# A hybrid streaming encoder step on one core: the order of TensorE's and ScalarE's work inside a mixer slot

## The chip, the core and the metric

One Trainium2 chip, and of it one core. The kernel is one program on that core: TensorE (PE) multiplies, VectorE (DVE) and ScalarE (ACT) work element by element, GpSimd (POOL) does a few additions, SyncE (SP) issues the transfers. Each engine runs its own list of instructions in order, and the lists are tied together by semaphores alone. The metric is the time of one execution in microseconds on the device; the kernel before has a median of 2633.47 us over 3 runs (2633.35 to 2634.78).

## What is computed

One trunk layer of an encoder for a prompt of 1024 tokens and a sample of 64 tokens (with caches). Cut to what matters here:

```python
x = x + 0.5 * swiglu_ffn(x, *ffn1)
h = rms_norm(x, mix_g)
qa, ka, va, qb, kb, vb, fl = split(h @ w_in)            # heads, q and k normalized per head
o_a = band_sink_attention(qa, ka, va, bias, valid, sink)  # 8 heads on 2 key heads, window of 3 chunks of 64
o_b = forgetting_attention(qb, kb, vb, F, F, pos, pos)    # 8 heads, causal, F = cumsum(log_sigmoid(fl + b_f))
g_a, g_b = split(sigmoid(h @ w_gate))
x = x + (g_a * (o_a @ w_a) + g_b * (o_b @ w_b)) @ w_out
x = x + 0.5 * swiglu_ffn(x, *ffn2)
x = x + sigmoid(rms_norm(x) @ w_pg) * (p @ w_pp)
```

Both attentions are a softmax over scores plus a bias (or decay), times values. Dimensions: model 1024, feed-forward 2816, head 64.

## The kernel before

Tokens lie along the free axis, 1088 of them in three chunks of 364, 364 and 360 columns. Every dense float32 product is made of three products of split operands (high by high, low by high, high by low). The program is a first feed-forward, then the **mixer**, then a merge, a second feed-forward and a last gate. Only the mixer is touched; it lies between about 838 and 1319 us of the profiled span.

In the mixer, projection weights come in units of 128 output columns. One chunk of a unit takes 24 products (`PRODUCTS`, 8 blocks of the model by 3 ways). The mixer is cut into **slots** (`N_SLOTS` = 86), and all engines walk through the slots in the same order, each with its own code per slot: `mix()` in the TensorE, ScalarE and VectorE parts, and a loop on SP. Tables made ahead (`TAKEN`, `ITEM_AT`, `TURN_AT`, `VALUE_AT`, `ST_AT`) say what a slot holds:

- **unit products** (L658): slots 0 to 5 have 24, slots 6 to 25 have 21 or 22, slots 26 to 67 have 15 or 16, slots 68 to 81 have 10 or 11, slots 82 to 85 none. Slots 68 to 81 make the first merge gates and are called the gate stage here.
- **scores** of one attention item (L688): item g stands in slot 6+g. Items 0 to 19 belong to the sliding window (four head pairs of five items; of the five the first has a narrow part, the last is the sample with 64 rows). Items 20 to 75 belong to the forgetting attention, 14 per head pair; an item has at most 512 keys, and a row block of 128 queries with more keys takes two items, of which the second closes the softmax.
- **turns** (L707 and L709): the weights of one item are transposed into PSUM, one slot after its scores in the sliding window (`LAG` 1), two slots after them in the forgetting attention.
- **value product** (L731): values times turned weights, in the slot behind the turns (`VALUE_AT` = turn slot + 1).
- in some slots a **head sum** for the norm of queries and keys (L749), or **turned values** (L757 to L763).

Between them stands other engines' work on the same item. VectorE adds the bias and takes the running minimum of the negated scores (L1277), ScalarE takes exponents (L976) when the item closes a softmax, VectorE scales by the inverse sum (L1306, semaphore `probs_done`), TensorE turns, ScalarE copies the turned weights to SBUF (`copies`, L925, semaphore `turn_done`), TensorE multiplies by the values (`pv_done`), and ScalarE copies a finished output (`outputs`, L990). For a head normalization ScalarE squares (L950), TensorE sums, ScalarE takes logarithm, exponent and square (`head_root`, L960 to L964), and VectorE finishes in three steps at the start of its next slot (L1241 to L1246), ahead of that slot's scores.

TensorE's order in a slot of the kernel before is: scores, half of the products, the value product of the turns of the slot before, head sum, the other half, this slot's turns, turned values. ScalarE's is: copies of the turns of the slot before, copy of the turned values of the slot before, square, exponents, root, output. TensorE asks for its banks and operands by waits:

```python
pe.wait_ge(turn_done, 2 * g + 2)      # value product: both copies of the turned weights
pe.wait_ge(probs_done, ...)           # turns: the scaled weights
pe.wait_ge(score_read, 2 * g)         # scores: the last scores have been read from the bank
```

## Time and profile before

| | kernel before |
|---|---|
| median of 3 runs | 2633.47 us |
| the profiled execution, own time | 2638.77 us |
| its span, first to last instruction | 2637.1 us |
| mean granted TensorE clock | 0.994 |
| TensorE busy | 2601.9 us, 99% |
| TensorE weight loads busy | 2450.6 us, 93% |
| VectorE busy | 1335.8 us, 51% |
| ScalarE busy | 722.6 us, 27% |
| GpSimd busy | 115.7 us, 4% |

The busy time of TensorE says that it almost always has a matmul in flight, not that it runs at its peak: matmuls overlap, and their ends are modelled. What an instruction occupies is read from the distance of its start to the next start. A row of the order of time gives start, duration (of all merged instructions), engine, source line, operation, output and inputs, shape, count, and in brackets the idle time before it and what ended it. Times count from the start of the span.

### The profile page before, as it was taken

To read this page: it belongs to the slowest core of one execution; us is meant where nothing else is said; L and a number is where in the kernel's file an instruction comes from. 1 tells how busy PE (TensorE), PEld (TensorE's weight loads), DVE (VectorE), ACT (ScalarE), POOL (GpSimd) and SP (SyncE) were. 2 spreads that over 40 slices of the span, in tenths; PEclk is the share of its full clock that TensorE was granted. 3 is DMA by queue.
4 is the path that set the end of the run, shared out by engine and by line. 5 is a ranking of instruction groups with operands and counts; after the bars stand their busy time and mean duration, and the time that the engine had idled before them with its cause. 6 is when DMAs were issued, how large, how long until landed. Compare 5 with 4: busy or idle time off the path is not lost.

```text
span 2637.1 us, 39357 instructions
## 1 busy us (share of the span) xinstructions
PE 2601.9 (99%) x15684; PEld 2450.6 (93%) x15684; DVE 1335.8 (51%) x2581; ACT 722.6 (27%) x1398; POOL 115.7 (4%) x156
## 2 busy tenths in 40 slices
PE   9999999999999899999999999999999999999999
PEld 9999999999998788777779989899999999999999
DVE  6444444444457675555433434554454444445664
ACT  5111111111124576555421111421111111111331
POOL 0000000000003000111100000300000000000210
PEclk9999999999999999999999999999999999999999
DMA  4111111111113211221131111111111111111112
GB/s 149 43 44 45 43 47 42 48 41 49 41 49 127 64 37 33 67 71 45 43 108 41 43 45 42 40 41 42 48 41 48 41 48 41 49 41 48 57 41 92
DMA packets 41677, 140.09 MB, mean 53 GB/s; under 512 B 5728, under 2 KB 8200, under 8 KB 41376
## 3 DMA queue, kind: packets, MB, share of 16 engines
q1 hardware_dynamic: 40944, 137.23, 16.5%
q8 instruction: 142, 2.33, 0.4%
q10 hardware_dynamic: 560, 0.28, 0.0%
q14 instruction: 31, 0.25, 0.0%
HBM read 122.91 MB, written 16.15 MB: 53 GB/s over the span
## 4 chain that ended last, share of the span: by engine, by line
PE 94%; DVE 3%; ACT 2%; issue 0%; ACTq 0%; DVEq 0%
PE psum L518 73%; PE psum L658 9%; PE psum L819 5%; PE psum L731 2%; PE psum L688 2%; PE psum L707 2%; PE psum L749 1%; ACT h_hi L864 1%; DVE w_lo L483 1%; ACT square L875 1%; DVE x L1177 0%; ACT w_hi L478 0%; DVE rstd L1129 0%; DVE ple_gate L1450 0%; ACT probs L976 0%
## 5 line engine op out<-in xcount | busy, mean ns | idle before, releaser
L518 PE MATMUL psum<-h_hi,w_hi 128*128 128x364 f32 (+1 forms) x2688 | 889.6, 331 | 14.6 <-DVE x L1177 10.7
L518 PE MATMUL psum<-h_hi,w_lo 128*128 128x364 f32 (+1 forms) x2688 | 885.7, 330 | 0.1
L518 PE MATMUL psum<-h_lo,w_hi 128*128 128x364 f32 (+1 forms) x2688 | 885.6, 329 | 0.0
L518 PEld LDWEIGHTS psum<-h_hi,w_hi 128*128 128x128 f32 x2688 | 507.4, 189 | 21.7 <-issue 10.2
L518 PEld LDWEIGHTS psum<-h_lo,w_hi 128*128 128x128 f32 x2688 | 507.1, 189 | 1.2
L518 PEld LDWEIGHTS psum<-h_hi,w_lo 128*128 128x128 f32 x2688 | 507.3, 189 | 0.0
L518 PE MATMUL psum<-hid_hi,w_hi 128*128 128x364 f32 x1296 | 425.9, 329 | 3.2 <-DVE hid_lo L1144 3.2
L518 PE MATMUL psum<-hid_lo,w_hi 128*128 128x364 f32 x1296 | 424.9, 328 | 0.0
L518 PE MATMUL psum<-hid_hi,w_lo 128*128 128x364 f32 x1296 | 424.5, 328 | 0.0
L1177 DVE SCALAR_TENSOR_TENSOR x<-psum,x 128x364 f32<-128x364 f32 (+1 forms) x624 | 318.8, 531 | 173.8 <-PE psum L518 173.4
L1138 DVE TENSOR_TENSOR pre<-psum,rstd 128x364 f32<-128x364 f32 x153 | 81.5, 535 | 393.0 <-PE psum L518 391.6
L478 ACT ACTIVATE w_hi<-w_raw 128x1024 fp32r<-128x1024 f32 x185 | 194.0, 1049 | 290.7 <-DMA w_raw<-w_units 290.7
L483 DVE TENSOR_TENSOR w_lo<-w_raw,w_hi 128x1024 fp32r<-128x1024 f32 x185 | 229.4, 1240 | 72.1 <-ACT w_hi L478 72.1
L518 PEld LDWEIGHTS psum<-hid_hi,w_hi 128*128 128x128 f32 x1296 | 243.2, 188 | 4.8 <-issue 4.3
L518 PEld LDWEIGHTS psum<-hid_lo,w_hi 128*128 128x128 f32 x1296 | 243.6, 188 | 0.4
L518 PEld LDWEIGHTS psum<-hid_hi,w_lo 128*128 128x128 f32 x1296 | 243.1, 188 | 0.0
L858 ACT ACTIVATE hid_hi<-prod 128x364 fp32r<-128x364 f32 x156 | 79.2, 507 | 534.3 <-DVE prod L1168 431.6
L892 ACT ACTIVATE sig<-pre 128x364 f32<-128x364 f32 x132 | 66.7, 507 | 553.2 <-DVE pre L1138 553.2
L1138 DVE TENSOR_TENSOR up<-psum,rstd 128x364 f32<-128x364 f32 x132 | 70.6, 535 | 248.9 <-PE psum L518 248.9
L658 PE MATMUL psum<-h_hi,w_hi 128*128 128x364 f32 (+1 forms) x456 | 159.7, 350 | 1.7 <-DVE q L1230 1.7
L658 PE MATMUL psum<-h_lo,w_hi 128*128 128x364 f32 (+1 forms) x456 | 157.9, 346 | 0.0
L658 PE MATMUL psum<-h_hi,w_lo 128*128 128x364 f32 (+1 forms) x456 | 156.8, 344 | 0.0
(137 smaller groups left out, 2127.4 us busy)
## 6 DMA issues: line engine op xcount, KB each, us to landing
w_raw<-w_units SPq DMA_DIRECT2D x193, 512.0 KB, 3.6
x<-x_t SPq DMA_DIRECT2D x8, 544.0 KB, 9.3
x_saved<-x SPq DMA_DIRECT2D x8, 544.0 KB, 5.4
x<-x_saved SPq DMA_DIRECT2D x8, 544.0 KB, 8.5
y_out<-x SPq DMA_DIRECT2D x8, 544.0 KB, 3.9
f_keys<-f_cumulative SPq DMA_DIRECT2D x4, 1024.0 KB, 6.4
f_samp<-f_cumulative SPq DMA_DIRECT2D x4, 576.0 KB, 7.1
kb_out<-k SPq DMA_DIRECT2D x4, 544.0 KB, 3.1
```

The costliest lines, as they stand in the source:

```text
L478: act.activation(w_hi[:, slot, :], w_raw[:, slot, :], ACT.Copy).then_inc(w_hi_done, 1)
L483: dve.tensor_tensor(w_lo[:, slot, :], w_raw[:, slot, :], w_hi[:, slot, :].bitcast(F32), ALU.subtract).then_inc(w_lo_done, 1)
L518: mm = pe.matmul(out, w[:, slot, w_cols], m, start=first and n == 0, stop=last and n == 2)
L658: mm = pe.matmul(psum[:, x % 2, 0:width], (w_hi, w_hi, w_lo)[way][:, slot, k * P:(k + 1) * P], (h_hi, h_lo, h_hi)[way][:, k, c0:c0 + width ...
L688: mm = pe.matmul(psum[0:rows, SC[h], at:at + width], q[hb:hb + HD, part["b"] * P:part["b"] * P + rows], keys, start=True, stop=True)
L707: mm = pe.transpose(out, cols, ident[0:rows, 0:rows])
L731: mm = pe.matmul(psum[hb:hb + HD, PV, col:col + rows], vals[0:width, hb:hb + HD], probs_t[0:width, h, j * P:j * P + rows], start=first, st ...
L819: mm = pe.matmul(psum[:, ev.mod(BANKS), 0:n], w_raw[:, slot, (4 * br + k) * P:(4 * br + k + 1) * P], o_t[:, 4 * br + k, c0:c0 + n], start= ...
L858: act.activation(hid[par][0][:, tile, c0:c0 + n], prod[:, (q + c).mod(2), 0:n], ACT.Copy).then_inc(hid_hi_done, 1)
L892: act.activation(sig[:, c0:c0 + n], pre[:, c0:c0 + n], ACT.Sigmoid).then_inc(sig_done, 1)
L1138: dve.tensor_tensor(out, psum[0:rows, e.mod(BANKS), 0:n], rstd[0:rows, c0:c0 + n], ALU.mult).then_inc(psum_free, 1)
L1177: dve.scalar_tensor_tensor(x[:, m, c0:c0 + n], psum[:, e.mod(BANKS), 0:n], half, x[:, m, c0:c0 + n], ALU.mult, ALU.add).then_inc(psum_free, 1)
```

## The change

In every slot that has unit products (`BUSY`, slots 0 to 81) TensorE's order becomes: scores, a quarter of the products, this slot's turns, products up to five eighths, head sum or turned values, the rest of the products, and then the value product of the turns of this same slot. ScalarE takes the copies of this slot's turns behind its exponents and ahead of the root, and the copy of turned values behind the root, in the same slot. In slots without products (82 to 85) the turns, copies and value products keep the old order. `values_product` asks for its values itself and returns the count reached. SP's wait on `pv_done` ahead of the next cached values goes with `VALUE_AT`, so it stands one slot earlier. No instruction is added or taken away.

```diff
--- before.py
+++ after.py
@@ -114,7 +114,6 @@
 LAG = {"a": 1, "b": 2}
 ITEM_AT = {DENSE + g: g for g in range(N_ITEMS)}
 TURN_AT = {DENSE + g + LAG[it["branch"]]: g for g, it in enumerate(ITEMS)}
-VALUE_AT = {slot + 1: g for slot, g in TURN_AT.items()}
 N_SLOTS = DENSE + N_ITEMS + 4
 EVACS = list(itertools.accumulate(it["out"] is not None for it in ITEMS))
 ROUNDS = list(itertools.accumulate(it["last"] for it in ITEMS))
@@ -146,6 +145,12 @@
 
 def slot_of(product):
     return next(slot for slot in range(N_SLOTS) if TAKEN[slot] > product)
+
+
+
+BUSY = [slot for slot in range(N_SLOTS) if TAKEN[slot] > (TAKEN[slot - 1] if slot else 0)]
+VALUE_AT = {slot if slot in BUSY else slot + 1: g for slot, g in TURN_AT.items()}
+assert len(VALUE_AT) == N_ITEMS
 
 
 
@@ -713,8 +718,9 @@
                 it = ITEMS[g]
                 rows = it["rows"]
                 v = UNIT_OF["va", 0] if it["branch"] == "a" else UNIT_OF["vb", it["pair"]]
-                if thirds:
-                    pe.wait_ge(values_done, thirds)
+                wanted = values_needed(g)
+                if wanted > thirds:
+                    pe.wait_ge(values_done, wanted)
                 if it["opens"] and EVACS[g - 1] and g:
                     pe.wait_ge(o_done, EVACS[g - 1])
                 if it["branch"] == "b" and it["values"][0][1][0] == "cache":
@@ -731,6 +737,7 @@
                         mm = pe.matmul(psum[hb:hb + HD, PV, col:col + rows], vals[0:width, hb:hb + HD],
                                        probs_t[0:width, h, j * P:j * P + rows], start=first, stop=last)
                 mm.then_inc(pv_done, 1)
+                return max(thirds, wanted)
 
             def sums_bank_free(slot):
 
@@ -772,21 +779,22 @@
                         wanted = norm_needed(g)
                         scores(g, wanted if wanted > need else 0)
                         need = max(need, wanted)
-                    unit_products(taken, taken + todo // 2)
-                    if slot in VALUE_AT:
-                        g = VALUE_AT[slot]
-                        wanted = values_needed(g)
-                        values_product(g, wanted if wanted > thirds else 0)
-                        thirds = max(thirds, wanted)
+                    if slot not in BUSY and slot in VALUE_AT:
+                        thirds = values_product(VALUE_AT[slot], thirds)
+                    first, second = taken + todo // 4, taken + 5 * todo // 8
+                    unit_products(taken, first)
+                    if slot in TURN_AT:
+                        turns(TURN_AT[slot])
+                    unit_products(first, second)
                     use = ST_AT.get(slot)
                     if use and use[0] == "sums":
                         head_sums(slot, use[1])
-                    unit_products(taken + todo // 2, taken + todo)
-                    taken += todo
-                    if slot in TURN_AT:
-                        turns(TURN_AT[slot])
                     if use and use[0] == "values":
                         turned_values(slot, use[2], use[3])
+                    unit_products(second, taken + todo)
+                    taken += todo
+                    if slot in BUSY and slot in VALUE_AT:
+                        thirds = values_product(VALUE_AT[slot], thirds)
 
             pe.wait_ge(set_up, 1)
             for _ in range(WARM_UP):
@@ -1002,17 +1010,19 @@
             def mix():
                 act.preload_act_table_set("natural_log_exp_and_others")
                 for slot in range(N_SLOTS):
-                    if slot - 1 in TURN_AT:
+                    if slot - 1 in TURN_AT and slot - 1 not in BUSY:
                         copies(TURN_AT[slot - 1])
-                    late, use = ST_AT.get(slot - 1), ST_AT.get(slot)
-                    if late and late[0] == "values":
-                        values_by_token(late[1])
+                    use = ST_AT.get(slot)
                     if use and use[0] == "sums":
                         head_square(use[1])
                     if slot in ITEM_AT and ITEMS[ITEM_AT[slot]]["last"]:
                         exponents(ITEM_AT[slot])
+                    if slot in TURN_AT and slot in BUSY:
+                        copies(TURN_AT[slot])
                     if use and use[0] == "sums":
                         head_root(use[1])
+                    if use and use[0] == "values":
+                        values_by_token(use[1])
                     if slot in VALUE_AT:
                         outputs(VALUE_AT[slot])
                     for n in range(3, len(MIX_UNITS)):
```

On TensorE, in slot 71 (item 65, 384 score columns, closing a softmax; eleven products), the kernel before has its value product (`psum<-probs_t,v_tok`) after five products:

```order
L658 MATMUL psum<-h_hi,w_hi 128x364
L658 MATMUL psum<-h_lo,w_hi 128x364
L731 MATMUL psum<-probs_t,v_tok_108 64x128 [waits turn_done,o_done,values_done]
L731 MATMUL psum<-probs_t,v_tok_108 64x128 x7
L658 MATMUL psum<-h_hi,w_lo 128x364
```

and its turns (`psum<-consts,probs`) after the last, with the next slot's scores behind them:

```order
L658 MATMUL psum<-h_lo,w_hi 128x364
L707 MATMUL psum<-consts,probs 128x128 [waits turn_done,probs_done]
L707 MATMUL psum<-consts,probs 128x128 x7
L688 MATMUL psum<-k_104,q_99 128x512 [waits score_read]
L688 MATMUL psum<-k_104,q_99 128x512
```

In the changed kernel the same slot has its turns after two products:

```order
L693 MATMUL psum<-k_104,q_99 128x384 [waits score_read]
L693 MATMUL psum<-k_104,q_99 128x384
L663 MATMUL psum<-h_hi,w_hi 128x364
L663 MATMUL psum<-h_lo,w_hi 128x364
L712 MATMUL psum<-consts,probs 128x128 [waits turn_done,probs_done]
L712 MATMUL psum<-consts,probs 128x128 x7
L663 MATMUL psum<-h_hi,w_lo 128x364
```

and the value product after the last, ahead of the next slot's scores:

```order
L663 MATMUL psum<-h_hi,w_hi 128x364
L663 MATMUL psum<-h_lo,w_hi 128x364
L737 MATMUL psum<-probs_t,v_tok_108 64x128 [waits turn_done,values_done]
L737 MATMUL psum<-probs_t,v_tok_108 64x128 x7
L693 MATMUL psum<-k_104,q_99 128x512 [waits score_read]
L693 MATMUL psum<-k_104,q_99 128x512
```

So turns and value product have changed places, and the value product now belongs to the turns of its own slot.

On ScalarE, in slot 14 (item 8 of the sliding window, with a head normalization), the kernel before has copies (`probs_t<-psum`), square, exponents (`probs,row_sum<-probs`), sink exponent, root in three steps, output:

```order
L925 ACTIVATE probs_t<-psum 128x512 [waits turn_full,pv_done]
L925 ACTIVATE probs_t<-psum 128x512 [waits turn_full]
L950 ACTIVATE head_sq<-q_103 128x360 [waits head_sum_full,pr_free]
L976 ACTIVATE probs,row_sum<-probs,neg_top 128x256 [waits score_read]
L976 ACTIVATE probs,row_sum<-probs,neg_top 128x256 x3
L982 ACTIVATE sink_exp<-sink_exp 128x4 [waits sink_sum]
L960 ACTIVATE y<-psum,eps 128x360 [waits normed,head_sum_full]
L962 ACTIVATE y<-y 128x360 [waits y_ready]
L964 ACTIVATE y_sq<-y 128x360 [waits y_ready]
L990 ACTIVATE o_t<-psum 128x512 [waits pv_done]
```

The changed kernel has there:

```order
L958 ACTIVATE head_sq<-q_103 128x360 [waits head_sum_full,pr_free]
L984 ACTIVATE probs,row_sum<-probs,neg_top 128x256 [waits score_read]
L984 ACTIVATE probs,row_sum<-probs,neg_top 128x256 x3
L990 ACTIVATE sink_exp<-sink_exp 128x4 [waits sink_sum]
L933 ACTIVATE probs_t<-psum 128x512 [waits turn_full,pv_done]
L933 ACTIVATE probs_t<-psum 128x512 [waits turn_full]
L968 ACTIVATE y<-psum,eps 128x360 [waits normed,head_sum_full]
L970 ACTIVATE y<-y 128x360 [waits y_ready]
L972 ACTIVATE y_sq<-y 128x360 [waits y_ready]
```

The copies have moved from ahead of the square to between the exponents and the root, and they are those of this slot's turns; the output, which is item 6's, now stands at the end of slot 13.

## Rows read from the trace of the kernel before

**Rows 1.** The page, busy time, share of the span and instructions of each engine:

```profile
PE 2601.9 (99%) x15684; PEld 2450.6 (93%) x15684; DVE 1335.8 (51%) x2581; ACT 722.6 (27%) x1398; POOL 115.7 (4%) x156
```

**Rows 2.** TensorE's waits: line waited for by: us in total, times, longest:

```profile
PE psum L731 <- ACT probs_t L925: 1.6, 3, 0.7
```

**Rows 3.** Stretches: length, busy (count) by engine, clock, DMA share, GB/s:

```profile
870.00:906.64 36.64, 29.31 (x181) 24.06 (x181) 24.54 (x78) 21.52 (x56) 0.00 (x0) 0.91 0.26 77
...
1020.60:1252.60 232.00, 232.00 (x1622) 179.27 (x1620) 125.56 (x339) 127.92 (x291) 32.24 (x54) 1.00 0.18 59
1252.60:1315.30 62.70, 62.21 (x464) 45.68 (x462) 29.31 (x91) 29.83 (x73) 7.94 (x16) 1.00 0.15 45
```

**Rows 4.** Order of time, TensorE, first scores of slots 12 and 17:

```profile
920.96 1.13 PE L688 MATMUL psum<-k,q 64*128 64x256 f32 x8
...
957.04 1.13 PE L688 MATMUL psum<-k,q 64*128 64x256 f32 x8
```

**Rows 5.** Order of time, VectorE, slots 14 to 16:

```profile
935.60 0.53 DVE L1241 SCALAR_TENSOR_TENSOR y_sq<-psum,y_sq 128x364 f32<-128x364 f32 x1
...
937.25 0.48 DVE L1277 CUSTOM_DVE_ANT_0 probs<-psum,bias,neg_sink 128x256 f32<-128x256 f32 x1
...
944.75 0.40 DVE L1277 CUSTOM_DVE_ANT_0 probs<-psum,bias,neg_sink 64x192 f32<-64x192 f32 x1
...
951.08 0.34 DVE L1277 CUSTOM_DVE_ANT_0 probs<-psum,bias,neg_sink 128x128 f32<-128x128 f32 x1
```

**Rows 6.** Order of time, ScalarE, slots 14 to 16:

```profile
935.09 1.06 ACT L925 ACTIVATE probs_t<-psum 128x512 f32<-128x512 f32 x2
...
938.99 0.51 ACT L976 ACTIVATE probs<-probs,neg_top 128x256 f32<-128x256 f32 x1 [2.44 <-DVE neg_top L1277]
...
941.07 0.54 ACT L960 ACTIVATE y<-psum,eps 128x360 f32<-128x360 f32 x1
...
942.18 0.51 ACT L964 ACTIVATE y_sq<-y 128x360 f32<-128x360 f32 x1
...
945.53 0.46 ACT L976 ACTIVATE probs<-probs,neg_top 64x192 f32<-64x192 f32 x1 [0.99 <-DVE neg_top L1277]
...
952.55 0.40 ACT L976 ACTIVATE probs<-probs,neg_top 128x128 f32<-128x128 f32 x1 [1.59 <-DVE neg_top L1277]
...
954.41 0.56 ACT L960 ACTIVATE y<-psum,eps 128x364 f32<-128x364 f32 x1
```

**Rows 7.** Order of time, TensorE, slot 71:

```profile
1266.66 0.92 PE L688 MATMUL psum<-k,q 64*128 64x384 f32 x4
1267.51 0.43 PE L658 MATMUL psum<-h_hi,w_hi 128*128 128x364 f32 x1
...
1268.52 1.09 PE L731 MATMUL psum<-probs_t,v_tok 128*64 128x128 f32 x16
1269.55 0.43 PE L658 MATMUL psum<-h_hi,w_lo 128*128 128x364 f32 x1
...
1270.65 1.03 PE L707 MATMUL psum<-consts,probs 128*128 128x128 f32 x8
```

**Rows 8.** Order of time, VectorE, slot 71, the first head's minimum:

```profile
1267.75 0.62 DVE L1277 CUSTOM_DVE_ANT_0 probs<-psum,f_keys,neg_top 128x384 f32<-128x384 f32 x1 [1.93 <-PE psum L688]
```

**Rows 9.** Order of time, ScalarE, slot 71, the first head's exponents:

```profile
1268.95 1.04 ACT L976 ACTIVATE probs<-probs,neg_top 128x896 f32<-128x896 f32 x1 [1.68 <-DVE neg_top L1277]
```

**Rows 10.** Order of time, TensorE, slots 7 to 9:

```profile
884.14 1.11 PE L761 MATMUL psum<-consts,v_t 128*128 128x128 f32 x4 [3.51 <-ACT v_tok L939]
885.18 2.08 PE L688 MATMUL psum<-k,q 64*128 64x256 f32 x8
...
895.52 1.13 PE L688 MATMUL psum<-k,q 64*128 64x256 f32 x8 [2.15 <-DVE neg_top L1277]
...
899.85 0.40 PE L658 MATMUL psum<-h_hi,w_hi 128*128 128x364 f32 x1 [1.67 <-DVE q L1230]
```

**Rows 11.** Order of time, ScalarE, the copies of slot 8's turns:

```profile
897.59 1.05 ACT L925 ACTIVATE probs_t<-psum 128x512 f32<-128x512 f32 x2
```

## Prediction

> **What bounds the kernel now.** I read the page first, then the waits of TensorE, then the busy time by stretches, then the order of time in single slots. TensorE is busy 99% of the span [rows 1], so an instruction on another engine costs nothing unless TensorE ends up waiting for it. In the whole span TensorE waits three times, 1.6 us in all, for the copies of turned weights (`probs_t`) [rows 2]. The stretches say the same: in the middle of the mixer (slots 26 to 67, 232 us) and in its gate stage (slots 68 to 81, 62.7 us) TensorE is busy all but 0.5 us; only in slots 6 to 9 it is not, 29.3 of 36.6 us, with a mean granted clock of 0.91 [rows 3]. So the old order hides all of the attention chain (scores, minimum, exponents, weights, turns, copies, value products) behind unit products. What has to be asked is what the new order leaves uncovered.
>
> **What moves.** No arithmetic is added or removed. The old order gave every hand-over most of a slot: turns at the end of slot s, their copies on ScalarE at the start of slot s+1, the value product after half of the products of s+1. Now turns, copies and value product stand in one slot. On ScalarE the copies move from ahead of the exponents to behind them; on TensorE the value product becomes the last thing of the slot, and the scores of the next slot are queued behind it. A new wait follows: value product on copies, copies behind exponents, exponents on VectorE's minimum, and that on this slot's own scores. Who is late if it is late: everything, since TensorE runs in order. Three prices follow from it, by stage, and one for the breaks in TensorE's stream. What else moves is covered: the copy of a finished output (`outputs`) now waits on ScalarE for the value product at the slot's end, and behind it stand a weight split and the next slot's exponents, which wait longer for scores and minimum (2.3 to 2.8 us, below) than the output takes; SP waits for that value product one slot earlier before it loads the next pair's cached values, with nothing urgent behind it; the turned values are copied in their own slot, which can only help the next user of their bank.
>
> **First, a ring in the sliding-window stage (slots 10 to 24).** Here nearly every slot has a head normalization. VectorE finishes the normalization of the slot before and then reads the scores: 935.60 to 937.25, 1.65 us [rows 5]. Scores to exponents take 937.25 to 938.99, 1.74; exponents to the logarithm 938.99 to 941.07, 2.08; the root's three steps 941.07 to 942.18+0.51, 1.62; then VectorE's next normalization [rows 6]. Without copies this ring is 1.65+1.74+2.08+1.62 = 7.09 us, and the old copies ran beside VectorE. The new order puts the copies between exponents and logarithm: 1.06 us [rows 6], of which I take 0.1 to lie under the instruction before or behind (an estimate); so 0.96, and 8.05 in all. For the five items of a head pair: two such slots; one with three quarters of the copies, 7.8; the short first item (951.08 to 952.55, 1.47, exponents to 954.41, 1.86, and copies of a 64-row item, estimated at half, 0.5), 7.1; the 64-row item (944.75 to 945.53, 0.78; exponents two of 0.46 and a small one, 1.1; full copies), 6.1 [rows 5, 6]. Sum 37.1. TensorE's five slots took 920.96 to 957.04, 36.08 us, without a wait [rows 4]. TensorE can't run ahead of this ring, because its value product waits for the copies in it. So 1.0 to 1.1 us per five slots, three times: **+3.3 us**. Bounds: 0 if small overlaps shorten the ring by 3%, +7 if each hand-over costs 0.1 us more.
>
> **Second, the gate stage (slots 68 to 81), where a slot has only ten or eleven products.** Worked for slot 71. Its scores start at 1266.66; the minimum starts at 1267.75 (+1.09 [rows 7, 8]), the exponents at 1268.95 (+1.20 [rows 9]); they are two of 1.04 [rows 9], with the sum's read-out 2.2; copies 1.06 [rows 6]. So the value product can start 5.5 us behind the scores. Ahead of it TensorE has scores 0.85, eleven products at 1.10/6 = 0.183, and turns 1.0 [rows 7]: 3.9 us. It waits 1.6 us, and nothing else can fill that. The other slots that close a softmax go by the same sum with their widths: an exponent of 256 columns takes 0.51 [rows 6] and one of 896 takes 1.04 [rows 9], so 128 columns are 0.11 for a head; narrower scores shorten score matmul and minimum alike; copies go with their columns. Estimated so: slot 69 1.4 (wider exponents, short copies), slot 73 1.3, slot 75 0.9, slot 76 1.4, slot 77 0.8. Together 7.4 us. The slots between have no exponents and wait for nothing. Without a head sum the last two stretches of products run as one; by my reading of the breaks (below) this gives back 0.09 in each of 14 slots, 1.2 us. **+6.2 us.** Bounds: +4 and +9.
>
> **Third, slots 26 to 67.** There are 15 or 16 products and in many slots a head sum, a slot is 232/42 = 5.5 us [rows 3], so most chains fit. Not all: where a normalization of the slot before stands ahead of a closing item (slot 35 and its like), the way from copies to copies is root 1.62, normalization 1.65, scores about 1.1, two exponents of 384 columns about 0.6 each, copies of one block about 0.5: 6.1 us, against about 5.2 of TensorE's own work there (a mean slot with fewer score columns): 0.9. Three further slots of 14 lack about 0.3. 1.8 less 0.4 given back by undivided products: 1.4 per head pair, three pairs: **+4.2 us**. Bounds: 0 (all covered) and 10.8 (four waits of 0.9 in each).
>
> **Start and end.** In slots 7 to 9 the forget gate's work on ScalarE and VectorE makes TensorE wait already: 3.51 us ahead of 884.14, 2.15 ahead of 895.52, 1.67 ahead of 899.85 [rows 10]. In the new order the first two change places with waits of value products on copies: the copies of slot 8's turns start at 897.59 [rows 11], end 1.05 later, and only then come value product (1.0) and scores of slot 9, 4.3 us later than 895.52. But the old order stands still until 899.85 anyway; following the chain to slot 10 leaves **+1.1 us** (0 to 4.3). In slot 0 the head sum now stands behind five eighths instead of half of the products, which cover some of its wait, and at the end one value product fewer is in the tail: **-0.5 us** in all (-1 to 0).
>
> **Breaks in TensorE's stream.** A slot had four changes of array shape (scores, value product in and out, scores again) and now has three, but the products are cut once more, by the turns. The five products from 1267.51, ahead of a value product, take 1.01 us; the six from 1269.55, ahead of turns, which have the products' own shape, take 1.10, or 0.92 for five [rows 7]. The 0.09 us between them is what I put on a change. The new entry from turns into products isn't in the trace; 0 and 0.2 us bound it. I take 0.1, so that a slot with a head sum or turned values comes out even, and one without gains 0.09 (counted above). Over 76 slots the bounds are -7 and +6 us.
>
> **Sum.** 3.3+6.2+4.2+1.1-0.5 = +14.3 us. The profiled execution took 2638.77 us (span 2637.1, 1.7 around it), so 2653.1 in its terms; the runs' median is 5.3 lower, 2633.47, which gives 2647.8, say **2648 us**.
>
> **Rivals.**
> *Faster by fewer shape changes.* If the copies always landed before TensorE comes to the value product, only the breaks would be left: 76 changes at 0.09, 7 us less, 2626.5. It decides where the chain of a closing slot is shorter than its cover; the rows of slot 71 say 5.5 against 3.9. The Trainium skill, "TensorEngine Tiling (Array Packing)", Key Properties, says that a change of tiling mode drains TensorE; by that rule alone this rival would hold, and the trace agrees that a change costs something, but little.
> *No change.* The waits are half of what I price (ring 0, middle 0 to 1, gates 5) and the changes of shape give back 3 to 5: 2633 to 2638.
> *The clock.* After the 3.51 us wait the scores of 885.18 took 2.08 us where those of 895.52 took 1.13 [rows 10]: half the speed, the lower of the granted clock's two levels (1.2 and 2.4 GHz), which is how the mean of 0.91 there comes about [rows 3]. If the new waits of 1 to 1.7 us bring the same in ten slots, at about 1 us each: 2658. Against it: the wait of 2.15 us ahead of 895.52 was followed by scores at full speed. The Trainium skill, "TensorE: Matmul & The Clock Gate", the section on HAM oscillation, warns that idle gaps between bursts bring the clock down again and again; by it this rival would be likelier than I make it.
> *The change isn't what it says.* The order of instructions shows that it is, in all slots with products; only the tail keeps the old order.
>
> **Chances.** Forecast (waits as priced, 2641 to 2656) 0.65; clock or costlier breaks, 2656 and more, 0.15; no change 0.13; faster 0.07. Slower by over 0.2% (5.3 us, about what a measurement of this kernel can tell) 0.80, within 0.2% 0.13, faster 0.07. The range reaches from 2637 (ring and middle covered) to 2661 (clock, or all breaks at their upper bound).
>
> **What the changed profile would show.** TensorE's waits for `probs_t` from 1.6 to 15 to 30 us, at some thirty places; slots 12 to 16 at 37 instead of 36.1 us; the gate stage at 69 instead of 62.7, with 1.6 us ahead of slot 71's value product; scores to scores on VectorE 8 us in a full slot. I am wrong if TensorE waits there under 5 us in all, or if the loss sits in waits of turns for weights, which I put at nothing: weights end before the next slot's first quarter.

## The result and the profile after

The changed kernel takes 2650.3 us (median of 4 runs, 2649.2 to 2651.64), the kernel before beside it 2633.61 (2633.35 to 2634.78): a ratio of 1.0063 with a 95% interval of 1.0045 to 1.0080, so 16.7 us slower. The profiled execution took 2651.03 us with a span of 2649.4, which is 12.3 us above the profiled execution of before.

The busy row of the changed kernel's page, to be read beside [rows 1]; TensorE's share lost a point:

```profile
PE 2590.2 (98%) x15684; PEld 2447.7 (92%) x15684; DVE 1336.7 (50%) x2581; ACT 719.6 (27%) x1398; POOL 116.8 (4%) x156
```

TensorE's waits inside the mixer (line waited for by: us in total, times, longest) answer [rows 2]. L737 is the value product, L712 the turns, L756 the head sum:

```profile
PE psum L737 <- ACT probs_t L933: 30.8, 33, 4.8
PE psum L712 <- DVE probs L1316: 2.0, 3, 0.9
PE psum L756 <- DVE k L1148: 1.5, 1, 1.5
```

The copied weights, 1.6 us of waiting before, are now 30.8 us at 33 places. Weights that VectorE has still to scale cost the turns 2.0 us. The busy time by stretches, cut at the same slots as [rows 3] (6 to 9, 26 to 67, 68 to 81):

```profile
867.57:906.29 38.72, 30.82 (x197) 25.49 (x196) 23.62 (x76) 21.84 (x58) 0.00 (x0) 0.87 0.24 72
1024.21:1259.06 234.85, 225.36 (x1611) 177.56 (x1609) 125.93 (x338) 125.70 (x291) 33.12 (x54) 1.00 0.18 58
1259.06:1327.78 68.72, 59.93 (x461) 45.21 (x459) 29.17 (x92) 29.12 (x72) 7.99 (x16) 1.00 0.13 41
```

The middle stretch shows something that the waits alone would hide: TensorE stood idle for 9.5 of its 234.85 us, and for none of its 232.00 before, but the stretch is only 2.85 us longer. The other 6.6 us were given back by something else. The same holds for the gate stage: 8.8 us idle against 0.5 before, and 6.4 us longer. What gave them back is the main question of the experiments.

Slot 71 shows the waiting in one place. TensorE's order of time there, to be read beside [rows 7]:

```profile
1274.99 0.92 PE L693 MATMUL psum<-k,q 64*128 64x384 f32 x4
...
1276.11 0.33 PE L663 MATMUL psum<-h_lo,w_hi 128*128 128x364 f32 x1
1276.28 1.03 PE L712 MATMUL psum<-consts,probs 128*128 128x128 f32 x8
1277.07 0.41 PE L663 MATMUL psum<-h_hi,w_lo 128*128 128x364 f32 x1
1277.31 0.33 PE L663 MATMUL psum<-h_hi,w_hi 128*128 128x364 f32 x1
...
1278.47 0.33 PE L663 MATMUL psum<-h_lo,w_hi 128*128 128x364 f32 x1
1280.55 1.09 PE L737 MATMUL psum<-probs_t,v_tok 128*64 128x128 f32 x16 [1.75 <-ACT probs_t L933]
1281.58 1.13 PE L693 MATMUL psum<-k,q 64*128 64x512 f32 x4
```

The value product starts 5.56 us behind the scores, and the eleven products and the turns ahead of it are done 1.75 us too early. In the sliding-window stage the ring is seen on VectorE (normalization, then scores), slots 14 and 15:

```profile
935.79 0.54 DVE L1251 SCALAR_TENSOR_TENSOR y_sq<-psum,y_sq 128x364 f32<-128x364 f32 x1 [0.49 <-ACT y_sq L972]
...
937.45 0.48 DVE L1287 CUSTOM_DVE_ANT_0 probs<-psum,bias,neg_sink 128x256 f32<-128x256 f32 x1
...
943.87 0.53 DVE L1251 SCALAR_TENSOR_TENSOR y_sq<-psum,y_sq 128x360 f32<-128x360 f32 x1 [0.48 <-ACT y_sq L972]
...
945.52 0.40 DVE L1287 CUSTOM_DVE_ANT_0 probs<-psum,bias,neg_sink 64x192 f32<-64x192 f32 x1
```

and on ScalarE (exponents, copies, root) between them:

```profile
939.18 0.51 ACT L984 ACTIVATE probs<-probs,neg_top 128x256 f32<-128x256 f32 x1 [2.55 <-DVE neg_top L1287]
...
941.26 1.06 ACT L933 ACTIVATE probs_t<-psum 128x512 f32<-128x512 f32 x2
942.22 0.55 ACT L968 ACTIVATE y<-psum,eps 128x360 f32<-128x360 f32 x1
...
943.34 0.50 ACT L972 ACTIVATE y_sq<-y 128x360 f32<-128x360 f32 x1
```

Scores to scores are 8.07 us (937.45 to 945.52), and each step of this ring starts where the one before it ends: scores 1.73 us, exponents 2.08, copies 0.96, root 1.62, normalization 1.65.

This table has the length of each stage of the mixer, from first scores to first scores in TensorE's order of time (slot 0 from the first product, the tail from the first matmul of slot 82 to the start of the last one); the last column is the median of the whole execution (of one run for "before, again"). The ratios given with the experiments go by runs of the kernel before taken beside each, with medians of 2633.4 to 2634.7 us. The kernels below it are those of the experiments; "before, again" is a second profile of the kernel before.

| us | slots 0–5 | 6–9 | 10–24 | 25 | 26–67 | 68–81 | tail | sum | time |
|---|---|---|---|---|---|---|---|---|---|
| before | 31.45 | 36.64 | 107.59 | 6.43 | 231.98 | 62.30 | 3.57 | 479.96 | 2633.6 |
| before, again | 31.42 | 36.67 | 107.67 | 6.43 | 231.98 | 62.30 | 3.40 | 479.87 | 2634.0 |
| changed | 29.43 | 38.72 | 111.69 | 6.23 | 234.85 | 68.72 | 3.04 | 492.67 | 2650.3 |
| old pairing from slot 68 | 29.43 | 38.75 | 111.75 | 6.23 | 234.96 | 59.69 | 3.77 | 484.59 | 2642.9 |
| value product one slot later | 29.39 | 34.23 | 111.81 | 7.36 | 231.86 | 61.49 | 3.65 | 479.80 | 2635.9 |
| copies ahead of exponents | 29.43 | 35.55 | 105.28 | 6.23 | 225.13 | 62.98 | 2.98 | 467.58 | 2624.5 |
| before, turns early | 29.87 | 35.03 | 111.72 | 6.42 | 238.98 | 63.10 | 4.80 | 489.93 | 2648.5 |
| before, value product last | 29.87 | 34.86 | 106.89 | 6.24 | 224.53 | 59.79 | 4.81 | 466.99 | 2624.5 |
| copies first, old pairing from 68 | 29.43 | 35.55 | 105.28 | 6.23 | 225.16 | 59.68 | 3.82 | 465.14 | 2622.3 |
| value product last, head sum later | 28.94 | 34.86 | 105.02 | 6.24 | 224.10 | 59.63 | 3.98 | 462.75 | 2620.5 |

### The profile page after: what moved, and what is told of

The parts are those of the page before. It is cut to its first block, busy times and chain, and to the rows that moved or that the text cites. A ratio compares the mean times of both kernels' runs of the same rounds, so it can differ in the third digit from the quotient of the medians.

```text
span 2649.4 us, 39357 instructions
## 1 busy us (share of the span) xinstructions
PE 2590.2 (98%) x15684; PEld 2447.7 (92%) x15684; DVE 1336.7 (50%) x2581; ACT 719.6 (27%) x1398; POOL 116.8 (4%) x156
## 3 DMA queue, kind: packets, MB, share of 16 engines
q1 hardware_dynamic: 40944, 137.23, 16.1%
## 4 chain that ended last, share of the span: by engine, by line
PE 86%; ACT 6%; DVE 5%; issue 2%; ACTq 0%; DVEq 0%
PE psum L523 72%; PE psum L827 5%; PE psum L663 4%; ACT probs L984 2%; DVE probs L1287 2%; PE psum L737 2%; PE psum L693 2%; ACT probs_t L933 1%; PE psum L712 1%; ACT h_hi L872 1%; DVE w_lo L488 1%; ACT square L883 1%; DVE y L1254 0%; DVE y_sq L1251 0%; DVE x L1187 0%
```

## The experiments

**Old pairing from slot 68.** One edit of the changed kernel:

```diff
-BUSY = [slot for slot in range(N_SLOTS) if TAKEN[slot] > (TAKEN[slot - 1] if slot else 0)]
+BUSY = [slot for slot in range(68) if TAKEN[slot] > (TAKEN[slot - 1] if slot else 0)]
```

From slot 68 on the value product then stands right behind the scores, and ScalarE's copies at the head of the next slot.

> The changed kernel with the new pairing only in slots 0 to 67; from slot 68 on the value product belongs to the turns of the slot before, stands ahead of the slot's products, and its copies stand on ScalarE at the head of the next slot. The turns stay behind the first quarter of the products everywhere. Theory: the gate stage alone comes back, from 68.7 to 61.5 to 63 us, and all else stays as in the changed kernel: 2643 to 2645. Rival (early turns or the cuts they make are the cost of the gate stage): it stays at 66 or more, 2647 to 2651.

Measured: 2642.86 us (1.0031, 1.0020 to 1.0042). The gate stage takes 59.69 us: the 6.4 us of loss come back, and the stage is 2.6 us shorter than in the kernel before. Some 0.6 of these 2.6 us is only moved: a small value product, of slot 67's turns, stands in slot 67 here and in slot 68 in the kernel before. In the same way that of slot 81 stands in the tail, which takes 0.7 us more than in the changed kernel. TensorE's idle time in the stage falls from 8.8 to 0.6 us, and the stages ahead of it stay within 0.11 us of the changed kernel. So the waits for the copies are the whole loss of that stage, and there is a gain under it that my expectation of 61.5 to 63 didn't have.

**Value product one slot later**, behind the first quarter of the next slot's products; ScalarE's copies stay behind the exponents:

```diff
-VALUE_AT = {slot if slot in BUSY else slot + 1: g for slot, g in TURN_AT.items()}
+VALUE_AT = {slot + 1: g for slot, g in TURN_AT.items()}
...
                     unit_products(taken, first)
+                    if slot in VALUE_AT:
+                        thirds = values_product(VALUE_AT[slot], thirds)
                     if slot in TURN_AT:
                         turns(TURN_AT[slot])
```

> The changed kernel with the value product moved to the next slot, behind its first quarter of products and ahead of its turns; the copies stay on ScalarE behind the exponents. Theory: two mechanisms part here. In the gate stage the copies have a quarter of a slot more, so the waits there go and the stage comes back from 68.7 to 62 or 63. In slots 10 to 24 the ring on ScalarE and VectorE (normalization, scores, exponents, copies, root) still has the copies in it, so its three to four us of loss stay, as a wait for scores' banks, queries or weights instead of the copies: slots 10 to 24 at 111 to 112. Sum 2637 to 2643. Rival (only TensorE's wait for the copies counts, there is no ring): both stages come back, 2632 to 2636. Rival (breaks): 2647 to 2651.

Measured: 2635.86 us (1.0006, 0.9997 to 1.0015), no change from the kernel before that can be told. The total lies below my 2637 to 2643, in the range of the rival without a ring. The stages say otherwise: the gate stage is back at 61.49, while slots 10 to 24 keep 111.81 us; what made the total smaller than I put it are slots 6 to 9 (34.23) and 26 to 67 (231.86). VectorE's scores of slots 14 and 15 there are again 8.09 us apart:

```profile
933.64 0.48 DVE L1285 CUSTOM_DVE_ANT_0 probs<-psum,bias,neg_sink 128x256 f32<-128x256 f32 x1
...
941.73 0.40 DVE L1285 CUSTOM_DVE_ANT_0 probs<-psum,bias,neg_sink 64x192 f32<-64x192 f32 x1
```

and what TensorE waits for here (905 to 1020 us) isn't the copies at all:

```profile
PE psum L737 <- ACT o_t L996: 4.7, 3, 1.9
```

TensorE now runs ahead of the ring until a value product that opens a new output (in slots 15, 20 and 25) asks for the bank whose last output (`o_t`) ScalarE, late, has not copied. So the ring is real and doesn't need TensorE in it: the place of the copies between exponents and root costs some four microseconds in slots 10 to 24, whichever wait collects them.

**Copies ahead of the exponents**, TensorE's order as in the changed kernel:

```diff
                     if use and use[0] == "sums":
                         head_square(use[1])
+                    if slot in TURN_AT and slot in BUSY:
+                        copies(TURN_AT[slot])
                     if slot in ITEM_AT and ITEMS[ITEM_AT[slot]]["last"]:
                         exponents(ITEM_AT[slot])
-                    if slot in TURN_AT and slot in BUSY:
-                        copies(TURN_AT[slot])
```

> The changed kernel with one edit on ScalarE: the copies of this slot's turns stand behind the square and ahead of the exponents, instead of behind them. TensorE's order is that of the changed kernel in every slot. Theory (value products wait for copies that are queued behind this slot's exponents): the value product then no longer hangs on this slot's scores, so TensorE's waits for the copied weights fall from 30.8 us to under 5, slot 71 from 6.58 back to about 5.0 us, the gate stage from 68.7 to 62 or 63, slots 10 to 24 from 111.7 to about 108; what can come in its place is turns waiting for their scaled weights, 0 to 8 us. Median 2632 to 2640. Rival (the loss is in the breaks and shape changes of TensorE's stream): nothing comes back, 2647 to 2651. Rival (turns at the quarter come too early for the weights): waits of turns for weights of 8 us or more, 2641 to 2646.

Measured: 2624.51 us (0.9963, 0.9949 to 0.9976), faster than the kernel before by 10 us and than anything I expected. The waits in the mixer:

```profile
PE psum L712 <- DVE probs L1316: 6.0, 7, 1.6
PE psum L737 <- ACT probs_t L933: 3.9, 3, 2.8
PE psum L693 <- DVE neg_top L1287: 1.6, 1, 1.6
```

The waits for copies fell as expected, from 30.8 to 3.9 us, and 6.0 us of waits for scaled weights came in their place. But every stage from slot 10 to 67 is now shorter than before the change: with the waits gone, TensorE's new order is worth 6.9 us in slots 26 to 67 alone. The rival "the loss is in the breaks" had even the sign wrong: the breaks of the new order are cheaper.

**The kernel before with the turns early**, nothing else:

```diff
-                    unit_products(taken, taken + todo // 2)
+                    unit_products(taken, taken + todo // 4)
+                    if slot in TURN_AT:
+                        turns(TURN_AT[slot])
+                    unit_products(taken + todo // 4, taken + todo // 2)
...
                     unit_products(taken + todo // 2, taken + todo)
-                    if slot in TURN_AT:
-                        turns(TURN_AT[slot])
```

> The kernel before with one edit: the turns stand behind the first quarter of the slot's products instead of behind the last; value product, copies and everything else keep their places. It shows what the early turns cost by themselves: one more cut in the products of each of 76 slots, and waits of the turns for weights that VectorE has not scaled yet. My prediction put the waits at nothing and the cuts at 0 to 7 us: 2633 to 2641, with under 3 us of waits for weights. Rival (weights come too late for a turn at the quarter): waits of 10 us or more on the scaled weights in the sliding-window and the gate stage, 2643 to 2652; in the changed kernel these waits would then be hidden behind those for the copies, since TensorE is late there already.

Measured: 2648.53 us (1.0053, 1.0037 to 1.0068). The number is the rival's, its reason isn't. In the mixer:

```profile
PE psum L707 <- ACT probs_t L926: 8.0, 9, 1.4
PE psum L707 <- DVE probs L1307: 3.6, 4, 1.6
```

Late weights hold the turns for 3.6 us, where I had put under 3 and the rival 10 or more; 2.6 of it is in slots 7 and 9, where TensorE waited before as well. The larger wait, 8.0 us, is one that no theory named: turns wait for the copies of the turns before them, whose bank they overwrite and which stand on ScalarE a slot later. Early turns are only to be had with early copies. The cut itself is cheap, as the rows of the changed kernel's slot 71 above show: from the turns' start to the second product behind them there are 1.03 us (1276.28 to 1277.31), and eight turns at 0.108 and one product at 0.166 are 1.03. In the changed kernel's other slots with eight such turns and no wait it is the same within 0.01 us. Turns of the products' own shape cost nothing among them but themselves.

**The kernel before with the value product last**, behind the turns. Nothing moves on ScalarE:

```diff
                     unit_products(taken, taken + todo // 2)
-                    if slot in VALUE_AT:
...
-                        values_product(g, wanted if wanted > thirds else 0)
...
                     if slot in TURN_AT:
                         turns(TURN_AT[slot])
+                    if slot in VALUE_AT:
...
+                        values_product(g, wanted if wanted > thirds else 0)
```

> The kernel before with one edit on TensorE: the value product of the turns of the slot before stands behind this slot's turns, last in the slot, instead of after half of the products. Turns, copies and all of ScalarE's order stay; the copies still have most of a slot, so nothing new is waited for in slots with products. Theory (what the change gave back lies in the shape changes around the value product): in the rows of the kernel before, a value product among products costs 0.09 us going in (257 instead of 166 ns from start to start), 0.09 coming out and 0.10 at the second product behind it (271 instead of 166), 0.29 in all; beside turns and scores it shares its changes with them and costs 0.09 more than they do alone, so 0.195 us come back in each slot with products, 8.2 in slots 26 to 67 (41 value products), 2.7 in the gate stage, 14 to 15 in all: 2618 to 2622 us, and TensorE's waits stay within 2 us of those of before. In slots 10 to 24 the ring of 7.1 us per full slot without copies may hold back a part of the 2.9 us there. Rival (my prediction's price, 0.09 for a change): 2627 to 2631. Rival (the gain of the version with early copies came from the early turns, not from the value product's place): 2632 to 2637.

Measured: 2624.5 us (0.9966, 0.9952 to 0.9979). Slots 26 to 67 are 7.45 us shorter (8.2 expected), the gate stage 2.51 (2.7 expected), both without new waits: 0.18 us for each of the 41 and 14 value products that are moved out of the products. Slot 71 there:

```profile
1256.78 0.33 PE L658 MATMUL psum<-h_lo,w_hi 128*128 128x364 f32 x1
1256.95 1.03 PE L707 MATMUL psum<-consts,probs 128*128 128x128 f32 x8
1257.91 1.09 PE L731 MATMUL psum<-probs_t,v_tok 128*64 128x128 f32 x16
1258.94 1.13 PE L688 MATMUL psum<-k,q 64*128 64x512 f32 x4
```

Between turns and scores the value product adds 1.03 us (1257.91 to 1258.94). Among products, in slot 71 of before, its row and that of the first product behind it are in [rows 7], at 1268.52 and 1269.55; the last two products ahead and the second behind were:

```profile
1268.10 0.33 PE L658 MATMUL psum<-h_hi,w_hi 128*128 128x364 f32 x1
1268.27 0.32 PE L658 MATMUL psum<-h_lo,w_hi 128*128 128x364 f32 x1
...
1269.82 0.33 PE L658 MATMUL psum<-h_hi,w_hi 128*128 128x364 f32 x1
```

From the last product ahead to the second behind that is 1.55 us, and two products alone take 0.33: the value product added 1.22. The difference, 0.19 us, is the price of standing in the wrong company. The other slots of this kind, fourteen in before, agree within 0.01 us. The total came out at 2624.5 instead of 2618 to 2622 because slots 10 to 24 gave back 0.7 instead of up to 2.9 (two head sums wait 1.5 us for squares, in slots 10 and 20), because the tail lost 1.2, and because 4.0 us of what the mixer gained is missing in the medians (below, under the clock).

**Copies first, and the old pairing from slot 68**, the two edits shown above together.

> The version with the copies ahead of the exponents, and from slot 68 on the pairing of before with the value product right behind the scores (as in the run that put the gate stage back). Theory (shape changes and waits add stage by stage): slots 0 to 67 as with the early copies, the gate stage at 59.7 to 60.5 instead of 63.0 us, since the turns' waits for weights there (about 1.3 us) and a change of shape go: 2620 to 2623 us. Rival (the value product right behind the scores meets its copies too early in this order): the gate stage stays at 62 or more, 2624 to 2627.

Measured: 2622.28 us (0.9956, 0.9942 to 0.9969); the gate stage takes 59.68, the stages ahead of it agree with the version with copies first within 0.03 us. Stages add. As in the other version with the old pairing, slot 81's value product stands in the tail, which takes 0.8 us more.

**Value product last, the head sum later**, and in the last slots the value product ahead of the turns again:

```diff
-                    unit_products(taken, taken + todo // 2)
+                    if not todo and slot in VALUE_AT:
...
+                    unit_products(taken, taken + 3 * todo // 4)
...
-                    if slot in VALUE_AT:
+                    if todo and slot in VALUE_AT:
```

> The version with the value product behind the turns, with two more edits on TensorE: the head sum stands behind three quarters of the products instead of half, and in the last slots, which have no products, the value product stands ahead of the turns again, as in the kernel before. Theory: in that version two head sums waited 1.5 us for squares that ScalarE had not finished (slots 10 and 20) and the tail took 1.2 us longer than before; both come back, and slots 10 to 24 go from 106.9 to about 105.3 us: 2621 to 2623. Rival (the later head sum delays root and normalization, and VectorE's ring holds the next slot's scores instead): 2624 to 2627.

Measured: 2620.53 us (2620.14 to 2621.11; 0.9952, 0.9938 to 0.9965), the fastest version of this study: 13.1 us below the kernel before (2633.6 in the same comparison) and about 30 below the changed one. Slots 10 to 24 take 105.02 us, and TensorE's waits for copied weights are those of the kernel before:

```profile
PE psum L731 <- ACT probs_t L930: 1.6, 3, 0.7
```

**The kernel before, again**, for a second profile.

> The kernel before, unchanged, for a second profile. The first profile belongs to an execution of 2638.77 us, 5.3 above the median, with 3.4 us at half of the clock in slot 0. If that stretch and others like it are what set that execution apart, slot 0 takes 9.2 us as in every other run instead of 10.8, the mean clock is 0.996 or 0.997 and the time is 2631 to 2635; if the difference lies outside the clock, slot 0 stays at 10.8 us or the mixer's stages differ by more than 1 us elsewhere.

Measured: 2633.96 us. Every stage repeats within 0.17 us, slot 0 included (8.44 and 8.41 us from its first product to slot 1's first, with the half clock again). So neither answer holds as I wrote it: the half clock in slot 0 came back, and the 4.8 us between the two executions lie outside the mixer: 1.2 ahead of it and 3.5 behind it (from the start of its last matmul to the end of the span 1318.6 and 1315.1 us). What brings the half clock in slot 0 stays open: the versions with the turns early and with the value product last have the same order there, wait the same 1.98 us, and take 6.85 us at the full clock. Behind the mixer the granted clock differs, in the ten microseconds that begin just before the mixer's end. First profile of before, second, and the changed kernel (the clock is the third number from the right):

```profile
1316.00:1326.00 10.00, 8.29 (x39) 5.24 (x39) 1.67 (x2) 5.89 (x14) 0.00 (x0) 0.66 0.39 127
```

```profile
1314.90:1324.90 10.00, 8.23 (x48) 5.40 (x48) 2.36 (x4) 5.85 (x14) 0.00 (x0) 1.00 0.45 142
```

```profile
1329.00:1339.00 10.00, 8.80 (x39) 5.54 (x40) 1.67 (x2) 5.26 (x11) 0.00 (x0) 0.66 0.45 164
```

A mean of 0.66 in ten microseconds is 6.8 us at the lower level (1.2 instead of 2.4 GHz), in which TensorE does 3.4 us less of its work. The second profile of before has none of it, and is 3.5 us shorter behind the mixer.

## Why the prediction was right, and which step failed

The direction, the mechanism and the total were right: 2648 forecast, 2650.3 measured, waits for `probs_t` 30.8 us at 33 places where I wrote 15 to 30 at thirty. The total owes something to luck, in two errors that cancelled: for slots 10 to 81 the sum has 16.1 us lost to the waits and the ring and 2.4 given back; measured were 23.4 us more idle time and 13.2 us more length, so 10.2 given back.

- **Ring, +3.3.** Measured +4.1. The ring itself was priced to 0.02 us: 8.05 worked out, 8.07 measured, and slots 12 to 16 take 37.22 (37.1 worked out). The rest is the third head pair: its last slot, 24, took 7.00 us in before where slots 14 and 19 took 7.61, and the ring makes it 8.15 all the same. The version with the value product one slot later shows the ring without TensorE's wait for the copies.
- **Gate stage, +6.2.** Measured +6.42. Idle time ahead of the value products of slots 69, 71, 73, 75, 76 and 77 was worked out as 1.4, 1.6, 1.3, 0.9, 1.4 and 0.8; from the starts of TensorE's instructions they are 1.6, 1.8, 1.4, 0.9, 1.4 and 0.9, and two more (78 and 81) add 0.9. So the waits were 1.5 us more than the 7.4 I had, and what was given back was 2.5 instead of 1.2. The old pairing from slot 68 takes all of it away.
- **Slots 26 to 67, +4.2.** Measured +2.85, with both parts too small. Per head pair I had 1.8 us of waits; the pair of slots 40 to 53 has 3.5, in five places (0.75, 0.54, 0.51, 0.74 and 0.99, the last in slot 49, the like of slot 35, put at 0.9). Against it I had 0.4 given back, and it is about 2.5.
- **Slots 6 to 9, +1.1.** Measured +2.1. The waits did change places as described: 4.8 us ahead of slot 7's value product, 2.1 ahead of slot 8's, and none ahead of slot 9's first products. (The upper bound is 4.1 by its own rows, not 4.3: 897.59, 1.05 and 1.0 make 899.64, against 895.52.)
- **Ends, -0.5.** Measured -2.6: the tail -0.54, and slot 0 -2.0. In slot 0 the wait is 0.5 us shorter; the other 1.5 or so is the clock, since the kernel before has 3.4 us of the lower level there in both of its profiles and none of the other versions has it. I had read the wait there, but not the clock behind it.
- **Waits of turns for weights, put at nothing.** Measured 2.0 us, in slots 7, 28 and 82: small, and not where the loss sits.
- **Breaks, about 0, bounds -7 and +6. This is the step that failed.** I priced a change of shape by one side only, 0.09 us, took 0.1 for the new entry from turns into products, and so let the extra cut eat what the value product's move gives back. The cut costs nothing (turns have the products' shape), and a value product among products pays at more places than the one: 0.09 going in (starts 0.25 apart instead of 0.166, 1268.27 and 1268.52) and 0.10 at the second product behind it (0.27 apart, 1269.55 and 1269.82). Coming out it pays the same in both places: from its start it is 1.03 us to the first product and 1.03 to the scores. By moving to the slot's end it saves 0.18 to 0.19 us, in every slot with a value product: slots 10 to 81 are 13.3 us shorter in the fastest version, whose waits there are those of before. My lower bound of -7 did not hold that. The rival that the change is faster by fewer shape changes was given 7 us; it was worth almost twice as much, and the version with the copies first is that rival come true: what stood against it was the place of the copies on ScalarE. The Trainium skill, "TensorEngine Tiling (Array Packing)", Key Properties, says that a change of tiling mode drains TensorE. The rows agree that a change costs time, more than the one step of 0.09 that I had looked at; that it is a drain they don't show.
- **The clock.** The rival of ten new falls did not come: from slot 10 to 81 the granted clock is 1.00 in every profile, in spite of 23.4 us of new waits of up to 1.8 us. The Trainium skill, "TensorE: Matmul & The Clock Gate", the section on HAM oscillation, tells of waits for transfers that are longer than these and that bring the clock down again and again. I read it as making this rival likelier, without asking how long its waits were; gaps of the size and number here did nothing.
- **From the profiled execution to the median, 5.3 us off for both kernels alike.** It held for before only, and the clock behind the mixer has a part in that. The mixer explains 12.7 of the 16.7 us between the medians, and the two profiled executions, both with the lower clock behind the mixer, differ by 12.3. About 3.4 of the remaining 4 is what that stretch costs, if most runs of before go without it, as its second profile does. Every profile of another order has the lower clock there, for 6.8 us (3.4 in the version with the value product one slot later), and each of those orders is missing something like it between mixer and median (1.3 us in that version, 2.2 to 4.1 in the others): the mixer is shorter by 12.4, 13.0, 14.8 and 17.2 us in the four faster versions, the medians by 10.2, 8.9, 11.2 and 13.1; with the turns early it is longer by 10.0, the median by 13.8. Slot 0 can be a part of it: if most runs of before go without the lower clock there too, 1.5 us of each of these differences is that; no run here shows it. That the unprofiled runs of before do without it is inferred from these times, not seen. What is on record of them, the mean clock of each whole execution, fits: the three of the 36 runs of before beside the experiments that took over 2636.5 us are the three with a mean of 0.994; the others have 0.995 to 0.998 (the second profiled run, with 0.994 and 2633.96 us, does not fit). But the clock isn't all: behind the mixer the version with the old pairing from slot 68 takes 1319.4 us, longer than the first profile of before (1318.6), with one fall of the clock fewer there. Why most runs of one order avoid the fall stays open.

## What to carry to other kernels

A producer and its consumer can share a slot only if the link between them on the other engine doesn't queue behind that same slot's own chain: the same order of TensorE is 17 us slower than the kernel before with ScalarE's copies behind the exponents, and 10 us faster with the copies ahead of them. Price a change of array shape on all its sides, from the last instruction ahead to the second behind, and put matmuls of odd shapes beside each other rather than among the long run. When a sum comes out right, look at whether its terms did: here idle time and stage lengths did not agree, and the difference, 10.2 us in slots 10 to 81, was four times what the sum had for it.

## What the runs showed that was not expected

- A value product of sixteen small matmuls costs 1.22 us among products and 1.03 us between turns and scores; turns among products cost nothing beyond their own 0.108 us each.
- Early turns by themselves made the mixer from slot 10 on 13.2 us longer, most of it not by late weights (1.0 us there) but by their own bank, which the copies of the turns before had not yet left (8.0 us).
- Up to 3.4 us of a run's time hang on whether 6.8 us behind the mixer run at the lower clock, in code that no version here touches; the mixer itself repeats within 0.1 us.
